# Diagonal blocks as 64x64 products and a half step on two-block matrices, with the first ada units moved up

## What is computed

```python
def trunk_layer(xc, xl, c, c_ctx, cos, sin, p, ctx_out):
    mod_l = jnp.split((jax.nn.silu(c) @ p['ada_w'] + p['ada_b'])[:, None, :], 6, axis=-1)
    hl = modulate(xl, p['norm1_g'], mod_l[0], mod_l[1])
    ... = split_cols(hl @ p['w_in'])          # rkv, wl, al, gl and the rest
    ...
def rwkv_inputs(rkv, wl, al, gl, p):
    ...
    w_pre = p['rwkv_w0'] + einsum(tanh(wl), p['rwkv_w2'])
    a = sigmoid(p['rwkv_a0'] + einsum(al, p['rwkv_a2']))
    g = jax.nn.sigmoid(gl) @ p['rwkv_g2']     # the gate of the branch's output
...
def step(S, inp):                              # 512 steps, both directions, 16 heads of 64
    rt, wt, kt, vt, at, bt = inp
    sa = einsum('dbhvk,dbhk->dbhv', S, at)
    S = S * wt[..., None, :] + sa[..., :, None] * bt[..., None, :] + vt[..., :, None] * kt[..., None, :]
    y = einsum('dbhvk,dbhk->dbhv', S, rt)
```

## Time and profile before

| | us |
|---|---|
| median of three runs | 2762.18 |
| lowest, highest | 2760.99, 2764.26 |
| the profiled execution | 2767.3 |
| its span | 2765.5 |
| PE busy in the span | 2694.9 |
| DVE busy | 1403.6 |
| ACT busy | 734.9 |
| POOL busy | 215.0 |

### The profile page before, as it was taken

One profiled execution on the slowest core, in us unless ns is written; L12 is line 12 of the kernel. 1 busy time (PEld: TensorE's weight loads), 2 busy tenths in 40 slices (PEclk: granted clock), 3 DMA queues, 4 the chain that ended last, 5 costly groups with the idle time before them and its releaser, 6 DMA issues.

```text
span 2765.5 us, 61050 instructions
## 1 busy us (share of the span) xinstructions
PE 2694.9 (97%) x26901; PEld 1733.2 (63%) x26901; DVE 1403.6 (51%) x2723; ACT 734.9 (27%) x1502; POOL 215.0 (8%) x184
## 2 busy tenths in 40 slices
PE   7999999999999999999999999899999999999999
PEld 3455555556444446748888444566666677787887
DVE  2676666674322233337778112777777633314541
ACT  3234333442222221111111003333443322211110
POOL 1000000000000002214444000000000000000000
PEclk9999999999999999999999999999999999999999
DMA  7211111111334333345533224212221233356554
GB/s 262 57 50 43 50 43 51 50 40 43 116 90 120 85 115 95 102 126 156 156 108 106 69 76 142 59 51 59 59 58 51 52 113 107 107 145 188 153 149 120
DMA packets 500007, 264.52 MB, mean 96 GB/s; under 512 B 42864, under 2 KB 493888, under 8 KB 499232
## 3 DMA queue, kind: packets, MB, share of 16 engines
q1 hardware_dynamic: 498016, 251.58, 31.3%
q0 software_dynamic: 1728, 9.03, 0.9%
HBM read 255.33 MB, written 5.24 MB: 94 GB/s over the span
## 4 chain that ended last, share of the span: by engine, by line
PE 92%; ACT 4%; DVE 2%; issue 2%; POOL 0%; DMA 0%; POOLq 0%; ACTq 0%; DVEq 0%
PE psum L515 35%; PE psum L517 14%; PE psum L1179 12%; PE psum L1291 8%; PE psum L779 2%; PE psum L549 2%; PE psum L1012 1%; PE psum L888 1%; PE psum L1000 1%; PE psum L590 1%; PE psum L990 1%; PE psum L729 1%; PE psum L769 1%; PE psum L756 1%; PE psum L902 1%
## 5 line engine op out<-in xcount | busy, mean ns | idle before, releaser
L515 PE MATMUL psum<-hT,strips 128*128 128x256 f32 (+1 forms) x2252 | 710.4, 466 | 1.2 <-issue 1.2
L515 PEld LDWEIGHTS psum<-hT,strips 128*128 128x128 f32 x2252 | 420.9, 192 | 229.6 <-issue 192.1
L517 PE MATMUL psum<-hT,strips 128*64 128x512 f32 (+1 forms) x1896 | 393.5, 535 | 2.6 <-DVE arena L2364 1.4
L1291 PE MATMUL psum<-arena,strips 128*128 128x512 f32 (+1 forms) x704 | 227.6, 486 | 0.6 <-DVE arena L2803 0.6
L1291 PEld LDWEIGHTS psum<-arena,strips 128*128 128x128 f32 x704 | 133.7, 190 | 93.0 <-issue 83.2
L517 PEld LDWEIGHTS psum<-hT,strips 128*64 128x64 f32 x1896 | 116.4, 136 | 108.5 <-issue 85.0
L515 PE MATMUL psum<-arena,strips 128*128 128x256 f32 (+1 forms) x416 | 125.9, 461 | 0.9 <-DVE done L2652 0.9
L2803 DVE SCALAR_TENSOR_TENSOR arena<-psum,mod,arena 128x256 f32<-128x256 f32 x24 | 10.9, 480 | 193.7 <-PE psum L1291 193.7
L515 PEld LDWEIGHTS psum<-arena,strips 128*128 128x128 f32 x416 | 78.9, 190 | 45.0 <-issue 36.8
L2185 DVE TENSOR_SCALAR arena<-arena 128x512 f32<-128x512 f32 (+1 forms) x88 | 69.7, 792 | 70.5 <-ACT arena L2040 68.1
L1179 PE MATMUL psum<-arena,rwkv_branch 128*128 128x256 f32 x424 | 99.0, 379 | 0.0
(11 more groups left out here) (303 smaller groups left out, 4166.9 us busy)
## 6 DMA issues: line engine op xcount, KB each, us to landing
strips<-in_w_in_dram SPq DMA_DIRECT2D x152, 512.0 KB, 3.8
strips<-in_ada_w_dram SPq DMA_DIRECT2D x80, 512.0 KB, 4.9
strips<-in_ffn_up_dram SPq DMA_DIRECT2D x46, 512.0 KB, 3.8
strips<-in_ffn_down_dram SPq DMA_DIRECT2D x32, 512.0 KB, 3.8
conv_branch<-in_ffn_up_dram SPq DMA_DIRECT2D x28, 512.0 KB, 4.8
arena<-in_ada_w_dram SPq DMA_DIRECT2D x4, 2048.0 KB, 14.6
strips<-in_w_in_dram SPq DMA_DIRECT2D x32, 256.0 KB, 3.4
strips<-in_a_out_w_dram SPq DMA_DIRECT2D x16, 512.0 KB, 3.8
```

What stands on the lines that cost most here:

```text
L515: return pe.matmul(o, lhs, rhs, start=start, stop=stop, skip_group_check=True)
L517: ins = pe.matmul(o[64 * h:64 * h + 64], lhs[:, 64 * h:64 * h + 64], rhs, start=start, stop=stop, skip_group_check=True)
L1291: ins = mm(s.o[:, lo:T], strip[:, b, j, :], hid[:, k, lo:T], k == 0, k == FT - 1)
```

## The change

- `diagonal_blocks` multiplies whole chunks: 32 matmuls of 64 rows, 64 weight columns and 64 moving columns, for four chunk pairs, two directions, two chunks of a pair (column half) and two heads (row half and bank). Of each 64x64 result only the two diagonal 32x32 blocks are kept.
- `turn_blocks` masks 1024 columns instead of 512 into a new view `LB` (the memory of `MV`, 16 slots of 64), and adds the two 32-column halves of each slot to get `LC` as before.
- POOL adds the unit diagonal to `LB`, 16x64 columns, instead of `LC`, 16x32.
- `half_step` multiplies 64x64 block-diagonal matrices: 32 matmuls of 64 rows, 64 weight columns and 32 moving columns.
- `diagonal_blocks(i + 1)` moves ahead of the last `fill`, right behind `outputs_of_states`.
- In layer 1 the gate's low-rank strip (`low2`) is computed for the last 256 columns alone, as are ACT's two operations on it.
- At the start `ada_unit(0)` comes right behind the input transposes, then `spread_tokens`, `turn_params`, `ada_unit(1)`, and both picks after that. SP loads the last two ada units after the first low-rank strip instead of after the third. DVE makes the spread rows after three of four input copies, and splits `scaled` in tiles 0 to 2 and 3 to 7 around the first gain.

```diff
-                    for b in range(2):
-                        for c in range(NCH):
-                            p, m = c % 2, c // 2
-                            for d in range(2):
+                    for m in range(4):
+                        for d in range(2):
+                            for p in range(2):
+                                c, n = 2 * m + p, (4 * d + m) * CH
                                 for h in range(2):
-                                    o = PS[quad(2 * p + b), b0 + h, (4 * d + m) * 32:(4 * d + m + 1) * 32]
-                                    ins = one(o, BK[d][rows(h), c, p, 32 * b:32 * b + 32],
-                                             ar[d][rows(h), c, 0, 32 * b:32 * b + 32])
+                                    ins = one(PS[rows(p), b0 + h, n:n + CH], BK[d][rows(h), c, p, :], ar[d][rows(h), c, 0, :])
...
                     for t in range(SLOTS):
-                        for q in range(4):
-                            ins = one(PS[quad(q), b0, t * 32:(t + 1) * 32], LC[quad(q), t, :], T16[quad(q), t, :])
+                        for p in range(2):
+                            ins = one(PS[rows(p), b0, t * 32:(t + 1) * 32], LB[rows(p), t, :], T16[rows(p), t, :])
...
                         if c == NCH - 1:
                             outputs_of_states(i)
+                            if ahead:
+                                diagonal_blocks(i + 1)
                         if c > 0:
                             fill(steps, hop)
...
-                    if ahead:
-                        diagonal_blocks(i + 1)
                     fill(steps, everything)
...
-                    pool.tensor_tensor(LC, LC, tab["unit32"].unsqueeze(1).broadcast_to([P, SLOTS, 32]), ALU.add)\
+                    pool.tensor_tensor(LB, LB, tab["unit64"].unsqueeze(1).broadcast_to([P, SLOTS, 64]), ALU.add)\
...
-                    tt(LC.rearrange("p (h s) t -> p h s t", h=2),
-                       PS[:, b0:b0 + 2, 0:256].rearrange("p h (s t) -> p h s t", t=32),
-                       tab["strict32"].unsqueeze(1).unsqueeze(1).broadcast_to([P, 2, 8, 32]), MUL).then_inc(s.free, 1)
+                    tt(LB, PS[:, b0:b0 + 2, :].rearrange("p h (s t) -> p (h s) t", t=64),
+                       tab["strict64"].unsqueeze(1).broadcast_to([P, SLOTS, 64]), MUL).then_inc(s.free, 1)
                     dve.wait_ge(*s.freed)
+                    t = did(tt(LC, LB[:, :, 0:32], LB[:, :, 32:64], ADD))
+                    dve.wait_ge(*t)
...
             def low_rank(l):
-                steps = fresh_strips([(A, ("low0", l)), (A, ("low1", l)), (G, ("low2", l))], 0, 2 * l)
+                steps = fresh_strips([(A, ("low0", l)), (A, ("low1", l)), (G, ("low2", l))],
+                                     (0, 0, 0 if l == 0 else SEG), 2 * l)
```

57 lines of the change are left out of this document (33 added, 24 removed).

## The result

The changed kernel takes **2797.36 us** (median of 4 runs, 2791.52 to 2801.28) against 2761.59 us for the kernel before in the same session (4 runs, 2760.08 to 2764.26). The ratio is **1.013, with a 95% interval of 1.0117 to 1.0144**: 1.3% slower. The direction was forecast; the forecast size was half of the measured one (+18 us forecast, +36 us between the medians), and 2797 lies just above the range, whose upper end was 2795.

What follows compares the result with a forecast made beforehand. TensorE (97% busy) and the chain from `turn_blocks` to the half step bound the kernel. 24.6 - 3.4 - 1.5 - 1.5 = +18.2 us gave a median of 2780 us (2785.5 profiled), 0.65% slower; range 2758 to 2795.

Steps and rivals of the forecast that it cites:

- Diagonal blocks and their place: TensorE's diagonal products, moved ahead of one dense step: four tiles overlap, 0.34 us less on TensorE, result 0.24 sooner.
- rival 4: The four tiles don't overlap in the new diagonal blocks, 1.88 us instead of 0.99: +14, 2794 us; chance 0.12.
- The chain's start: VectorE's chain from turn_blocks starts 1.24 us sooner in layer 0, 0.91 in layer 1, about 2.4 in three blocks there.
- The chain's growth: VectorE's chain to the half step: mask +0.52, new addition +0.73, standing still for POOL's longer addition +1.29, together +2.54 us.
- Rival 1: POOL's longer addition doesn't hold VectorE longer, so the chain grows by 1.25 only: +3.6, 2766 us; chance 0.12.
- The half step: TensorE's 32 larger products cost their 64 weight columns, 1.88 us instead of 1.21: +0.67 for each block.
- Rival 2: In the half step, 64 weight columns cost nothing over the 32 moving ones: +4.6, 2767 us; chance 0.11.
- rival 3: VectorE's chain grows by less than its earlier start and margin, so TensorE never waits: -10, 2752 us; chance 0.09.
- The sum over blocks: Over both layers' blocks, chain growth less earlier start and margin, plus the half step's 0.67 each: +24.6 us.
- The gate's strip: Layer 1's low-rank gate strip: eight TensorE products of 256 columns fall away, -3.4 us.
- The start: Before the first dense strip, TensorE's 0.71 us idling and first pick leave the chain to the gain: -1.5 us.
- Stops without releaser: TensorE stops that no engine ends: one more spared besides three in layer 1's diagonal blocks, -1.5 us, ends 0 and -5.

Runs made afterwards that it cites:

- a1: Changed kernel with POOL's unit addition on 1 of 16 slots (64 columns instead of 1024), other slots' unit diagonal left out: 2750.29 us.
- p1: Kernel before with only layer 1's gate strip cut to the last 256 columns: 2758.99 us, ratio 0.9973 to 0.9990.
- p2: Kernel before with only the new order of the start: 2762.54 us, ratio 0.9993 to 1.0010.
- p3: Kernel before with only the 64 old diagonal products moved ahead of the dense step: 2762.48 us, ratio 0.9987 to 1.0006.
- c1: Changed kernel with the old half step and POOL's 512-column unit addition released later, beside a mask that reads PSUM: 2745.5 us, ratio 0.9921 to 0.9948.
- a3: Changed kernel with more dense work placed ahead of the half step, taken from behind it: 2772.49 us, ratio 1.0023 to 1.0049.
- d1: Whole changed kernel with POOL's unit addition released later, at the first pairs' mask that reads PSUM: 2784.22 us, ratio 1.0072 to 1.0100.
- a4: Kernel before with three idle 512-column tensor operations added to VectorE's turn_blocks, TensorE's program unchanged: 2800.3 us, ratio 1.0124 to 1.0154.
- a2: Changed kernel with the old half step (64 products of 32x32) and POOL's addition on 512 columns again: 2746.9 us, ratio 0.9933 to 0.9966.
- d2: c1 with eight more 256-column products ahead of each half step of layer 1, taken from behind it: 2748.78 us, ratio 0.9945 to 0.9973.

## Why the prediction was right in direction and wrong in size

By its own steps, each with what the traces showed:

- **Diagonal blocks and their place.** From the start of `outputs_of_states` to the first of L930 (L932) in block 1 of layer 0 it was 177.75 to 182.73, 4.98 us; it is 181.99 to 186.42, 4.43. That is 0.55 less for the block, where 0.34 was forecast: besides the products themselves, at the forecast 0.9 to 1.0 us, the dense step is no longer cut in two. The four tiles overlap, so rival 4 falls; the last result is there after 1.20, against a forecast of 1.16.
- **The chain's start.** Measured against `outputs_of_states`, the mask starts 1.36 us sooner in layer 0 (4.18 before, 2.82 now) and 1.04 in layer 1; forecast 1.24 and 0.91.
- **The chain's growth.** 15.73 to 18.06, +2.33, forecast +2.54. The mask and the addition have their forecast lengths (1.22 and a step of 0.73). POOL's addition takes 2.38, not 2.58, for twice the columns, and L2421 grew by 1.10 instead of 1.29. Rival 1 falls by this, and a1 shows the cause. The Trainium skill ("SBUF — State Buffer", section "SBUF: two separate sides") has this as an exclusive lock for the whole instruction; the 2.72 and 0.65 us of L2421 agree.
- **The half step.** 202.93 to 204.91, 1.98 us to the next instruction against 1.21: +0.77, forecast +0.67. 32 pairs of records at 0.062: the weights' 64 columns count, not the 32 moving ones. Rival 2 falls, and with both of its conditions rival 3.
- **The waits.** 0.95 to 1.06 us in layer 0 and 1.78 to 1.83 in seven blocks of layer 1, forecast about 0.8 and 1.6 to 2.
- **The sum over blocks.** With the measured terms: layer 0, blocks 1 to 7, 2.33 - 1.36 - 0.83 + 0.77 = 0.91 each, 6.4; layer 1, 2.33 - 1.04 + 0.77 = 2.06, three times, 6.2; block 6 with its margin 1.0; the three with a stop of 1.3 on average (3.9 in three) 2.3. In block 0 of layer 0 the wait went from 2.47 to 5.00; with 0.77 and the 0.3 saved, 3.0. In block 0 of layer 1 the half step has no wait; the one at L781 went from 1.5 to 2.3: 0.8 + 0.77 - 0.3 = 1.3. Together 20.2, forecast 24.6.
- **The gate's strip.** -3.4, as forecast (3.41 in p1).
- **The start.** -1.5 forecast, p2 shows no difference. The first strip (L551) does come 2.8 us sooner, at 28.37 instead of 31.14.
- **Stops without releaser.** This term was mis-sized by a factor of eight: -1.5 forecast, besides the three in the diagonal blocks (3.9 us). Measured 22.2 to 6.3, so -12.0 besides these three. What they waited for is shown below: blocks of TensorE's own instructions.
- **The granted clock.** The step that failed: the sum had no such term. A wait was priced at its own length, as if work behind it ran at the speed of before. Measured +22.0.

These give 20.2 - 3.4 - 12.0 + 22.0 = +26.8, and the profiled executions differ by 26.5. Against the forecast of +18.2 that is -4.4 in the blocks, -10.5 in the stops, +1.5 at the start and +22.0 by the clock. Errors of opposite sign stood behind it, and it is luck that they took away a good half of the largest. The medians differ by more, 35.8, since the profiled execution of before was 5.7 above its median and that of after 3.6 below. The granted clock of after in its four runs was 0.986, 0.987, 0.983 and 0.983; a change of 0.003 in it is 8 us of 2792, so most of the spread of 10 us between them goes with the clock. The kernel before spreads in the same way: over 4 us in the four runs beside the changed kernel, but over 12 (2757.4 to 2769.0, clock 0.997 to 0.992) in the 29 beside p1 to p3 and c1.

That the waits bring the clock down rests on four runs: a1 and a3 take the waits away with the half step's products in place, d1 takes them away in one layer only, and a4 puts them into the kernel before, without touching TensorE's program. The Trainium skill ("TensorE: Matmul & The Clock Gate", section "A second HAM failure mode: psum-queue depth-cycling") describes a kernel whose engine idles briefly between groups of matmuls and whose clock swings between the two levels, which costs throughput between the bursts; the ten stretches of after that stand at waits for VectorE are of this kind, though the waits here stand 61 to 78 us apart. Had this been a rival with a price, the row for it was there: the kernel before has three 1.2 GHz stretches in layer 1, and each begins within 2 us of a stop of TensorE (3.61, 1.59 and 1.46 us). In the trace of before, the window behind a stop of 3.61 us at 1771.7 (L826) reads:

```profile
1770.00:1781.00 11.00, 9.28 (x91) 7.11 (x91) 5.19 (x7) 6.02 (x10) 0.00 (x0) 0.54 0.01 1
```

What stays open: which of several equal waits is followed by the lower level. In the kernel before block 0's wait of 2.47 us is not; in a1 one of 2.8 is. In the changed kernel three of the seven waits of 1.0 in layer 0 are; of a4's five of 1.6 in layer 0 also three, at other blocks, and of its two of 0.9 and 1.0 none. A forecast can give this only as a share of the waits.

The stops follow the number of TensorE's instructions in most runs: 16.2 to 22.2 us in before and the four kernels with 26901 records, 9.1 to 13.5 in a2, c1 and d2 with 1000 fewer, 5.6 to 7.5 in after, a1 and d1 with 2048 fewer. a3 breaks the order, with 11.9 at 24893. They lie nearly all in layer 1's scan, where the products are shorter, and the one of 3.3 us stands at the same product (L826 to L828) in seven kernels.

What they waited for stands in the trace, among the DMA packets. The page has a queue of kind "instruction" (packets, MB, share); of before, then of after:

```profile
q8 instruction: 214, 3.51, 0.5%
```

```profile
q8 instruction: 198, 3.24, 0.5%
```

Its packets have 16384 bytes each. The change takes 4096 instructions from TensorE and 16 packets from this queue, which is 64 bytes for an instruction and 256 instructions for a packet, so it carries TensorE's program. Take the stop of the earlier trace rows, from 1932.16 to 1933.61: a packet starts at 1931.20 and lands at 1932.16, and TensorE goes on 1.45 us later. So it is everywhere: in the twelve traces all 117 stops over 0.5 us in the two scans end 1.2 to 1.7 us behind the landing of such a packet, where 7% of all products of layer 1's scan in before start 1.1 to 1.7 us behind one. The reading is that TensorE stood still because its next instructions were not there yet; it rests on these times, and no run moved the packets alone. The rows also suggest where that can happen: from the packet's start to the first product are 2.4 us at that stop, and the 128 records of the old diagonal blocks, which with their loads are 256 instructions, are gone through in 1.33 us. This would also let a3 have more stops than the changed kernel with the same products: while TensorE waits, packets can catch up, and a3 took those waits away. No run tries that by itself.

The Trainium skill ("Runtime: NRT & Kernel Launch", section "Instruction fetch mechanics") holds that the crossing from one block of instructions to the next is mostly hidden. Here 22 us of stops behind such packets are not hidden in before, and 6 in after.

## What to carry to other kernels

Price a new wait of the busiest engine at its own length and, where waits like these (1.0 to 1.8 us) will recur, add a term for the clock that falls behind them: here 22 us of waits brought 22 us more, in a4 27 us brought 14. Where an engine's stops have no releaser, lay its instruction queue's packets beside them. When a part is computed in larger pieces to spare instructions, ask who must prepare the larger operand; here 32 products less in the half step asked POOL for 512 more columns, and VectorE and TensorE paid for it. And try the parts apart: everything but the half step was worth 0.5%, and the half step hid it.

## What the runs showed of the hardware that was not expected

- Waits of 1.0 to 1.8 us, once per block of 61 to 78 us, were followed by the granted clock's lower level at eight of 14 half steps of after; all of the seven waits of 1.5 in d1 were (41 us at that level), of the seven of 1.8 in after only five (34 us), in one execution each. Waits of 0.1 to 0.2 us in a3 and d1 brought no such stretch in layer 0's blocks.
- With 2048 records and as many weight loads less on TensorE (7.6%), 16 us of stops that no engine had ended were gone. Each stop over 0.5 us ended 1.2 to 1.7 us behind the landing of a packet with TensorE's next 256 instructions. The products' own times didn't show it.
- POOL's addition took 1.29 us for 512 columns and 2.38 for 1024, 0.32 for 64; VectorE's operation of 0.48 us then took 1.62, 2.72 and 0.65. VectorE's time is POOL's plus 0.33 each time.
- A pair of records with 64 weight columns and 32 moving columns takes 0.062 us on two tiles, as one with 64 and 64 (0.059).
